# One mixer of a decoder trunk rewritten (V stationary, outputs by features, probabilities scaled on GpSimd), and the last four experts reordered

## The reference, cut to what matters

```python
def mixer_c(hn, w_in, b_in, sinks, w_out, b_out, cos, sin):      # 16 query heads of 64, 4 key/value heads, window 128
    q, k, v = jnp.split(hn @ w_in + b_in, [1024, 1280], axis=-1)
    q, k = rope(q), rope(k)
    s = einsum(q, k_band) * 64 ** -0.5                             # two blocks of 128 queries, band of 256 keys
    m = maximum(max(s), sink)
    p = exp(s - m)
    p = p / (sum(p) + exp(sink - m))
    o = einsum(p, v_band)
    return o @ w_out + b_out

def hierarchical_moe(x, ...):                                     # per token: one group of 8 experts, 2 experts in it
    h = silu(xb @ w_gate[e]) * (xb @ w_up[e])                     # 1024 -> 512, for the tokens of expert e
    y[token] += gate * (h @ w_down[e])                            # 512 -> 1024

h = x
for layer in range(2):
    h = h + mixer(rms_norm(h))
    h = h + hierarchical_moe(rms_norm(h))
out = rms_norm(h)
```

## Time and profile before

| what | value |
|---|---|
| median of 3 runs | 1198.61 us (1196.28 to 1199.93) |
| the profiled execution | 1199.88 us, of which the span of the trace is 1198.1 us |
| busy share: PE, PEld, DVE, ACT, POOL | 69%, 36%, 13%, 13%, 3% |
| DMA: bytes, mean rate over the span | 438.00 MB, 366 GB/s |
| mean granted clock of TensorE | 0.844 of full speed |
| chain that ended last | DMA 46%, PE 40%, issue 7%, DVE 3%, SP's queue 2% |

### The profile page before, as it was taken

The page is one execution under the profiler, slowest core; times in us unless marked ns, Lnnn a source line. Parts: engine busy times, 40 slices in busy tenths (PEclk is TensorE's granted clock), DMA queues, the critical chain, the costliest instruction groups (busy, mean ns, idle before and its releaser), DMA issues.

```text
span 1198.1 us, 12598 instructions
## 1 busy us (share of the span) xinstructions
PE 828.7 (69%) x5278; PEld 426.5 (36%) x5278; DVE 161.7 (13%) x422; ACT 150.0 (13%) x323; POOL 41.7 (3%) x52
## 2 busy tenths in 40 slices
PE   7999889473747464756599898765656564656565
PEld 6555684131313131313154587313222222222223
DVE  1142331000000000000023634000000000000003
ACT  2245131000000000000020423000000000000002
POOL 0010110000000000000001102000000000000000
PEclk9999999786968696869699999977787787777788
DMA  9941757999999999999998444999999999999991
GB/s 382 422 153 71 281 211 305 409 430 427 427 427 428 428 427 429 428 428 428 427 421 330 156 175 177 380 428 428 428 426 428 428 427 428 429 428 428 429 427 51
DMA packets 34557, 438.00 MB, mean 366 GB/s; under 512 B 3921, under 2 KB 3921, under 8 KB 8529
## 3 DMA queue, kind: packets, MB, share of 16 engines
q1 hardware_dynamic: 33936, 434.92, 86.7%
q10 hardware_dynamic: 576, 2.44, 0.5%
HBM read 436.30 MB, written 1.05 MB: 365 GB/s over the span
## 4 chain that ended last, share of the span: by engine, by line
DMA 46%; PE 40%; issue 7%; DVE 3%; SPq 2%; ACT 1%; POOL 1%; POOLq 0%; DVEq 0%; ACTq 0%
PE bank L1051 18%; DMA ring<-in_w_up 17%; DMA ring<-in_w_gate 14%; DMA ring<-in_w_down 14%; PE bank L810 9%; PE bank L948 4%; PE bank L838 3%; SPq L404 2%; PE bank L1027 2%; PE bank L789 1%; PE bank L1109 1%; PE bank L1085 1%; PE bank L959 0%; PE bank L873 0%; ACT arena L754 0%
## 5 line engine op out<-in xcount | busy, mean ns | idle before, releaser
L1051 PE MATMUL bank<-ring,hg 128*32 128x512 f32 x1792 | 288.1, 728 | 291.0 <-DMA ring<-in_w_up 82.8
L1051 PEld LDWEIGHTS bank<-ring,hg 128*32 128x32 f32 x1792 | 75.3, 131 | 482.5 <-issue 369.0
L1051 PE MATMUL bank<-arena,hg 128*32 128x512 f32 x256 | 142.6, 721 | 0.0
L1051 PE MATMUL bank<-ring,arena 128*32 128x512 f32 x704 | 111.5, 660 | 37.3 <-DMA arena<-in_w_down 20.0
L810 PE MATMUL bank<-ring,hg 128*128 128x512 f32 x256 | 112.4, 595 | 0.0
L1535 DVE TENSOR_TENSOR arena<-arena,bank 128x512 f32<-128x512 f32 x16 | 11.0, 688 | 564.4 <-PE bank L1051 564.4
L810 PEld LDWEIGHTS bank<-ring,hg 128*128 128x128 f32 x256 | 47.9, 190 | 56.4 <-issue 55.3
L1051 PEld LDWEIGHTS bank<-ring,arena 128*32 128x32 f32 x704 | 32.5, 119 | 98.9 <-issue 86.5
L1027 PEld LDWEIGHTS bank<-arena,hr 128*128 128x128 f32 x512 | 62.3, 202 | 14.0 <-issue 11.7
L1027 PE MATMUL bank<-arena,hr 128*128 128x128 f32 x512 | 65.3, 289 | 2.0 <-DVE arena L1505 2.0
L1051 PE MATMUL bank<-arena 128*32 128x512 f32 x192 | 63.9, 637 | 1.4 <-ACT arena L696 1.4
(11 more groups left out here) (182 smaller groups left out, 567.1 us busy)
## 6 DMA issues: line engine op xcount, KB each, us to landing
ring<-in_w_up SPq DMA_DIRECT2D x56, 2048.0 KB, 21.9
ring<-in_w_gate SPq DMA_DIRECT2D x50, 2048.0 KB, 20.0
ring<-in_w_down SPq DMA_DIRECT2D x48, 2048.0 KB, 19.9
arena<-in_w_down SPq DMA_DIRECT2D x14, 2048.0 KB, 27.7
arena<-in_w_up SPq DMA_DIRECT2D x8, 2048.0 KB, 28.8
arena<-in_w_gate SPq DMA_DIRECT2D x8, 2048.0 KB, 28.4
ring<-w_ab SPq DMA_DIRECT2D x6, 2048.0 KB, 30.2
ring<-in_w_gate SPq DMA_DIRECT2D x6, 1536.0 KB, 15.4
```

What stands on the lines that cost most here:

```text
L1051: op = pe.matmul(dst[rows, :], lhsT[:, q, rows], unit[s][:, q, cols], start=(q == 0), stop=(q == steps - 1))
```

## The change

**Mixer C.** The values matmul now has V stationary (64 columns for each head of the pair, side by side in the array) and the turned probabilities moving, so that its output lies by features and goes straight to `attT`: `c_o`, the turns of the outputs and their copies fall away. Since the division can't follow by rows any more, the probabilities are scaled before the turn: DVE makes the inverse for each pair (`inverse`), POOL scales the pair's probabilities (`normalise`, four `tensor_scalar` operations of 128x128 or 128x256 with one factor per row), and `c_p` gets four buffers. The copies of the turned probabilities are split between ACT (even heads) and DVE (odd heads), out of one bank; ACT copies each pair's output (`attended`). Every pair's output is one chunk of the output projection's inner dimension: `out_chunk` does its 8 matmuls between the steps of the next pair, and only the last pair's 8 are left for `out_proj_high`. The banks are moved accordingly, and SP fetches unit 6 of the next quad earlier in its queue (it now waits for the fourth pair's chunk), ahead of two parked units.

**Experts.** In the last quad, `combine` and `last_weights` come ahead of the up stage, which is run as two experts and then two. The routing saves one matmul and one DVE step; `gather` signals each half by itself. The bias rows are fetched in the mixer's loads, after its first weight unit.

```diff
+                if u == 1:
+                    for dst, src, n in ((sinks_b[:], sinks, SWA_HEADS), (c_bin, b_in_c, C_IN * HALF)):
+                        sp.dma_start(dst, row_bcast(src, n)).then_inc(rows_in, 16)
...
             park(1, 0)
+            sp.wait_ge(cc["used"], C_UNITS - 1)
+            first(1, 6)
             sp.wait_ge(cc["scores"], SWA_HEADS)
             park(1, 1)
             sp.wait_ge(cc["p_turned"], SWA_HEADS)
             park(1, 2)
-            sp.wait_ge(cc["used"], C_UNITS - 1)
-            first(1, 6)
             sp.wait_ge(cc["out"], KD)
...
+            def normalise(pair):
+                pool.wait_ge(cc["inverse"], pair + 1)
+                for t in (2 * pair, 2 * pair + 1):
+                    for b, cols in enumerate((slice(0, P), slice(P, TRI))):
+                        op = pool.tensor_scalar(c_p[:, t % 4, cols], c_p[:, t % 4, cols], c_den[:, t, b:b + 1], None, ALU.mult)
+                    op.then_inc(cc["p_scaled"], 1)
...
+                if u == 1:
+                    normalise(0)
+                    normalise(1)
+            for pair in range(2, SWA_HEADS // 2):
+                normalise(pair)
...
-                copy_hidden(last)
                 act.wait_ge(m["pickT"], n)
                 for pair in range(2):
-                    op = act.activation(last_wT[pair], bank[7][:, pair * S:(pair + 1) * S], ACT.Copy)
+                    op = act.activation(last_wT[pair], bank[5][:, pair * S:(pair + 1) * S], ACT.Copy)
                 op.then_inc(m["pickT_sb"], 1)
+                copy_hidden(last)
...
+            def copy_even(pair):
+                act.wait_ge(cc["p_turned"], 2 * pair + 1)
+                if pair > 0:
+                    act.wait_ge(cc["o"], pair)
+                act.activation(c_pT[:, 0, :], bank[C_TURN_BANK][:, 0:TRI], ACT.Copy).then_inc(cc["pT_even"], 1)
+
+            def attended(pair):
+                act.wait_ge(cc["o"], pair + 1)
+                act.activation(attT[:, pair, :], bank[C_VALUE_BANK][:, 0:S], ACT.Copy).then_inc(cc["att"], 1)
...
+            probs(0)
+            probs(1)
+            copy_even(0)
+            attended(0)
+            for pair in range(2, SWA_HEADS // 2):
+                copy_even(pair - 1)
+                probs(pair)
+                attended(pair - 1)
+                if pair == 3:
+                    turn_in(cc["q_turned"], 2, c_qT[1], (4, 5), -(HD ** -0.5), cc["q"])
+            copy_even(SWA_HEADS // 2 - 1)
+            attended(SWA_HEADS // 2 - 1)
...
-                pe.matmul(ranked[:, 0], before, one[0], start=False, stop=True, skip_group_check=True)
-                pe.matmul(ranked[:, 1], before, one[1], start=False, stop=False, skip_group_check=True)
-                pe.matmul(ranked[:, 1], ones[:], one[0], start=False, stop=True,
+                one = chosen.rearrange("p b g e -> p (b g e)")
+                ranked = bank[FREE_BANKS[l][0]][:, RANKS:RANKS + NB * EXPERTS]
+                pe.matmul(ranked, before, one, start=False, stop=False, skip_group_check=True)
+                pe.matmul(ranked[:, EXPERTS:NB * EXPERTS], ones[:], one[:, 0:EXPERTS], start=False, stop=True,
                           skip_group_check=True).then_inc(once["ranked"], 1)
...
+                    for high in range(2):
+                        for k in range(4):
+                            for b in range(NB):
+                                op = pe.matmul(of_block(bank[4 + high], k), hr[:, b, 4 * high + k, :], pick[:, b, :],
+                                               start=(b == 0), stop=(b == NB - 1))
+                        op.then_inc(m["gathered"], 1)
...
+                    if final:
+                        combine(i)
+                        last_weights()
+                        four(place, 1, bank[7], xeT, KD, slice(0, DE), strips=(0, 1))
+                        four(place, 1, bank[7], xeT, KD, slice(0, DE), strips=(2, 3)).then_inc(m["used"], 1)
+                    else:
+                        four(place, 1, bank[7], xeT, KD, slice(0, DE)).then_inc(m["used"], 1)
...
-                    if not first:
+                    if not first and not final:
                         combine(i, first=second)
-                    if final:
-                        last_weights()
...
+            def turn_p(t):
+                pe.wait_ge(cc["p_scaled"], t + 1)
+                if t == 0:
+                    pe.wait_ge(cc["k"], 1)
+                elif t % 2:
+                    pe.wait_ge(cc["pT_even"], t // 2 + 1)
+                else:
+                    pe.wait_ge(cc["pT_odd"], t // 2)
+                for j in range(3):
+                    op = turn(of_block(bank[C_TURN_BANK], j), c_p[:, t % 4, j * P:(j + 1) * P])
+                op.then_inc(cc["p_turned"], 1)
...
+                pe.wait_ge(cc["pT_even"], pair + 1)
+                pe.wait_ge(cc["pT_odd"], pair + 1)
+                heads = [(bank[C_VALUE_BANK][s * HD:(s + 1) * HD, 0:S], c_pT[:, s, :]) for s in range(2)]
+                for dst, pT in heads:
+                    pe.matmul(dst, c_v[:, 0, cols], pT[:, 0:S], start=True, stop=False, skip_group_check=True)
+                for dst, pT in heads:
+                    op = pe.matmul(dst[:, P:S], c_v[:, 1, cols], pT[:, S:TRI], start=False, stop=True, skip_group_check=True)
+                op.then_inc(cc["o"], 1)
...
+            def out_chunk(pair, lo, hi):
+
+                part, c = divmod(pair, 4)
+                if lo == 0:
+                    pe.wait_ge(cc["att"], pair + 1)
+                if pair == 0 and lo == 0:
                     pe.wait_ge(cc["biased"], 3)
...
+                if c == 0 and lo == 0:
+                    pe.wait_ge(w_landed[AB_UNITS - RING + 3 + part], 32)
+                return out_proj(1, attT, slot_out(c_slot(3 + part)), part, [4 * k + c for k in range(lo, hi)])
...
+            high_q(0, 6)
+            turn_q(0)
+            high_q(6, 8)
             swa_scores(0)
...
+            high_q(12, 14)
             turn_p(0)
-            high_q(12, 16).then_inc(cc["used"], 1)
+            high_q(14, 15)
+            turn_p(1)
+            high_q(15, 16).then_inc(cc["used"], 1)
             swa_scores(2)
-            turn_p(1)
             swa_values(0)
...
+            for pair in range(1, SWA_HEADS // 2):
+                if pair == 3:
+                    turn_q(1)
+                elif 1 < pair < SWA_HEADS // 2 - 1:
+                    swa_scores(pair + 1)
+                out_chunk(pair - 1, 0, 3)
+                turn_p(2 * pair)
+                if pair == 3:
+                    swa_scores(4)
+                out_chunk(pair - 1, 3, 6)
+                turn_p(2 * pair + 1)
+                op = out_chunk(pair - 1, 6, KD)
+                if pair == 4:
+                    op.then_inc(cc["used"], 1)
+                swa_values(pair)
+            pe.wait_ge(cc["att"], SWA_HEADS // 2)
+            out_proj_high(1, attT, slot_out(c_slot(4)), cc["out"], range(3, 4))
...
-                link(rank_of_pass(0))
...
+            def copy_odd(pair):
+                dve.wait_ge(cc["p_turned"], 2 * pair + 2)
+                if pair > 0:
+                    dve.wait_ge(cc["o"], pair)
+                dve.tensor_copy(c_pT[:, 1, :], bank[C_TURN_BANK][:, 0:TRI]).then_inc(cc["pT_odd"], 1)
+
+            def inverse(pair):
+                hs = slice(2 * pair, 2 * pair + 2)
+                dve.wait_ge(cc["prob"], 2 * pair + 2)
+                dve.wait_ge(cc["sink_exp"], pair + 1)
                 link(dve.tensor_tensor(c_den[:, hs, :], c_den[:, hs, :], c_sum[:, hs, :], ALU.add))
...
+                dve.reciprocal(c_den[:, hs, :], c_den[:, hs, :]).then_inc(cc["inverse"], 1)
...
+            masked_pair(0)
+            masked_pair(1)
+            inverse(0)
+            copy_odd(0)
+            inverse(1)
+            add_bias(2)
+            masked_pair(2)
+            copy_odd(1)
+            inverse(2)
+            add_swapped(2)
+            for pair in range(3, SWA_HEADS // 2):
+                masked_pair(pair)
+                copy_odd(pair - 1)
+                inverse(pair)
+            copy_odd(SWA_HEADS // 2 - 1)
...
```

240 lines of the change are left out of this document (63 added, 177 removed).

## The result

The changed kernel takes 1178.15 us, median of 4 runs (1176.60 to 1182.45), the kernel before 1199.27 us, median of 4. The ratio is 0.9843, 95% interval [0.9814, 0.9873]. By the medians the change gives 21.1 us, by the ratio 18.8 (15.2 to 22.3), where 21.2 was forecast. The execution whose profile follows is the slowest of the four, 1182.45 us with a span of 1180.6, so the two profiles lie 17.5 us apart.

The account below looks back on a forecast made before the run. Loads were taken to bound the experts and PE the second mixer. Gains of 1.3 + 1.84 + 10.8 + 7.3 = 21.2 us took the profiled 1199.88 to 1178.7, and 1.3 less for the median gave 1177.4; range 1173 to 1182, with rivals 1172 to 1190.

Parts of the forecast that it names:

- Part 1: Routing of each layer: one matmul and one DVE step fewer, gather signalled by halves; 1.3 us gained together.
- Part 2: Bias rows moved out of layer 0's saturated stretch into the mixer's loads: their bytes' time, 1.84 us, gained.
- Part 3: Last quad of each layer, combine ahead of up in halves: 5.5 us in layer 0, 5.3 in layer 1, together 10.8.
- it lands at about 1170.6: Layer 1's last load, needed by the second down part, read from a DMA share of 0.15 between 1170 and 1172.
- Part 4: Second mixer, PE's new order laid out with old durations: 7.3 us gained.
- the fill: Mixer's start, up to the first output's copy at 675.8: PE waits 1.8 us for POOL before the first turn.
- the tail: Mixer's end, last output's copy to last logits: two chunks take 1.87 us, last chunk's logits start at 726.6.
- The allowance of 0.5 for the clock: Mixer: 0.5 us taken off the gain for two waits in the fill, which may lower PE's clock.
- (a): Rival, mixer: POOL sets the round at 1.17 us or more per scaling; time 1183, or about 1194; chance 0.2.
- (b): Rival, mixer: POOL so slow, from 1.7 us an operation, that the whole change loses; 1209 at 2.0; chance 0.07.
- (c): Rival, last quad: halves give nothing; half the gain, 1183, chance 0.1; a loss, 1206, chance 0.02.
- The price on POOL: Mixer: POOL's scaling of a pair, two operations of 128x128 at 0.45 us and two of 128x256 at 0.72, takes 2.35.

Follow-up runs that it names:

- a_dve: The changed kernel with the probabilities scaled on DVE instead of POOL; 1176.52 us, ratio 0.9818.
- a_fill: The changed kernel with DVE's inverse of the first pair put ahead of the second pair's masks; 1176.30 us, ratio 0.9819.
- x_route: The kernel before with only the routing edits (one matmul and one DVE step fewer, gather signalled by halves); 1195.86 us, ratio 0.9964.
- x_rows2: The kernel before with the bias rows and sinks fetched a second time inside layer 0's saturated stretch; 1201.76 us, ratio 1.0014.
- a_whole: The changed kernel with the last quad's up stage in one piece of four strips instead of two halves; 1180.32 us, ratio 0.9852.
- a_pool2: The changed kernel with every scaling on POOL done once more into a scratch tile; 1195.13 us, ratio 0.9967.
- x_rows: The kernel before with only the bias rows moved, fetched behind the mixer's first weight unit; 1194.45 us, ratio 0.9953.
- x_mixer: The kernel before with only the second mixer rewritten, SP's order included; 1190.24 us, ratio 0.9921.

## Why the prediction was right, and which of its steps were not

- **The time** is right, 1178.15 against 1177.4, and that it is so near is in part luck. The sum of terms is right only in part: by the two profiles it is 17.5, by the ratio 18.8, not 21.2, and in it two terms too large by 3.3 and a term of 1.3 that came to -0.3 stand against one too small by 1.2. The forecast took 1.3 us for the way from the profiled execution to the median; in the changed kernel it is 4.3, and that closes the gap. Why it is so large I can only argue: a_dve and a_fill, with the same routing code, have 11.9 to 12.0 us in places where the changed kernel's profile has 13.2, 2.5 of the 4.3 us.
- **Part 1, routing (1.3).** "That is 0.57 us; layer 0 ... about 0.75." At like clock the edits give 12.53 to 12.0 or 13.6 to 13.2, 0.4 to 0.6 a layer, so the steps were about right. What the step left out is that PE's clock moves the same stretch by up to 2.9 us (10.40 to 13.28 with one code). In layer 1 it took the gain back (-0.67); in x_route it may have added 2 us to it.
- **Part 2, bias rows (1.84).** The bytes were right and the hole in the rate behind them was missed, though a window of 4 us at 232 in the profile before shows it: 3.0 in the profile, 3.6 over thirteen stages. The second fetch of x_rows2 cost 2.3 without a hole, so what makes the hole is open. The new place costs nothing, as forecast.
- **Part 3, last quad (10.8).** The order of work was right to about a microsecond: gate to first down part was laid out as 20.5 us and took 20.15, of which the last 0.5 is a wait for a load that the layout doesn't have. The step that failed is "it lands at about 1170.6", read from a DMA share of 0.15 in the earlier trace rows. In the profile after, the share is 0.67, 0.25 and 0 in the three windows that lead to the wait; a low mean share is some engines still at work, and the unit was there at 1159.0, after all of them. The profile before had the answer: its last down unit was issued at 1143.8 and took 28.7 us, so it landed at 1172.5, not 1170.6. The second down part came 29.8 us behind the gate instead of 28.5: 8.6 in all. "Any further speed of PE here would be lost to that load" fits a_whole, where a slower PE loses next to nothing.
- **Part 4, mixer (7.3).** The rounds were right (42.2 of 42.1). The two ends were not: the fill by 0.6, since POOL takes 2.98 and not 2.35 for a pair and 3.95 for its second pair, beside DVE's two-input operations (the forecast allowed 0.3 for that; the two operations that met them took 0.98 and 0.88 longer); the tail by 0.8, since PE takes its instructions in order and the wait for ACT's scaled chunk stands ahead of the next chunk's matmuls. The allowance of 0.5 for the clock stood for a fall that comes or not, and is worth 1.7 us when it comes; the profile before has one in this stage and the profile after none. 103.8 against 102.3 laid out.
- **The rivals.** (a) POOL at 1.17 us an operation: no, 0.60 and 0.92; the row of 1.165 with 16 elements misled, and what makes it dear isn't known. (b) The crossing "from 1.7 us for each operation on (6.7 a pair)" comes near to what a_pool2 gives, 6.5; and the mixer's loss laid out for a pair of 6.2, 9.8 us, is near the 9.7 that a_pool2's mixer lost at 5.95 (119.68 against 110.00). (c) Four fifths of the last quad's gain came.
- **The price on POOL.** The upper rate was taken from `tensor_tensor` 128x256 at 0.72; one-input 128x256 is 28% dearer, and 128x128 is not 0.45 but 0.60, or 0.72 in the mean with the two that DVE held up.

The four parts alone come to 0.47, 0.44, 0.79 and 0.36%, 2.06 together, against 1.57 [1.27, 1.86] for the whole. Added as squares the intervals of the parts give 0.41, which with the whole's own 0.30 just allows for the difference, but all four parts were compared with the same runs of the kernel before, so their errors are not independent. Why each of three parts gave more by its ratio than its own stages show (x_rows, x_mixer, x_route) is open; that x_route's gain needs the old mixer's dense tail in front of it is one reading, and no run tells it apart.

## What to carry to other kernels

When PE waits at the end of a layer for a load and has work of the previous step left, put that work ahead of the wait; then ask at once what is next, here the last load, and stop there. Read the landing of a transfer from its issue and its time to landing, or from a wait of its consumer, not from a low mean share of the DMAs. Before a chain of small steps on another engine ends in a run of matmuls, look at the clock of those matmuls in several profiles; a few matmuls into a bank that nobody reads can be worth more than a step saved in the chain.

## What the runs showed of the hardware

- A fetch of one 6 KB row into all 128 partitions (768 KB) cost a saturated stretch 3.6 to 3.8 us, twice its share of bytes, with a window of 4 us at 282 to 327 GB/s as it lands; a second one in the same stretch cost 2.3 and left no such hole. Between the mixer's loads it cost nothing that shows.
- Before the change the last 2 MB unit of layer 1 landed 28.7 us after its issue, though the mean share of the DMAs read 0.15 in the two us before; in the changed kernel it was 28.4.
- POOL's multiply by a factor per row took 0.60 us for 128x128 and 0.92 for 128x256, DVE's 0.28 and 0.35. By these the slope is 2.5 ns an element against 0.5. Two operations of 128x128 that met a two-input operation of DVE (128x512, 128x1024) took 1.58 and 1.48 us; the other fourteen took 0.60.
- The gather's 32 matmuls took 3.83 us at full clock and 5.2 to 6.7 where it fell; five matmuls of 128x256 in each routing kept it up in both layers.
- The same mixer code took 110.0 to 113.8 us in five profiles, with a fall of the clock in each and the longest fall in the longest mixer.
